# GpSimd's adds for the sums of squares, cut from one of 1280 columns into eight of 160

## The reference

```
h = rms_norm(x, norm1)
proj = h @ w_in                       # queries, keys, values, gates of three mixers
mix = concat(A(proj), B(proj), C(proj))   # sparse attention, band attention, SSD scan
x = x + mix @ w_out
u = relu(rms_norm(x, norm2) @ w_up)
x = x + (u * u) @ w_down              # d_ff = 8192
```

```
y = x32 * lax.rsqrt(jnp.mean(x32 * x32, axis=-1, keepdims=True) + EPS)
```

## Time and profile before

| | |
|---|---|
| runs, median of three | 3264.46 us |
| profiled execution, first to last instruction | 3258.3 us |
| TensorE matmul busy | 3122.3 us (96%) |
| VectorE busy | 1711.3 us (53%) |
| ScalarE busy | 1151.3 us (35%) |
| GpSimd busy | 135.7 us (4%) |
| TensorE's granted clock, mean | 0.978 |
| mean DMA rate | 136 GB/s |

### The profile page before, as it was taken

The page is one execution under the profiler, slowest core; times in us unless marked ns, Lnnn a source line. Parts: engine busy times, 40 slices in busy tenths (PEclk is TensorE's granted clock), DMA queues, the critical chain, the costliest instruction groups (busy, mean ns, idle before and its releaser), DMA issues.

```text
span 3258.3 us, 54928 instructions
## 1 busy us (share of the span) xinstructions
PE 3122.3 (96%) x20829; PEld 3064.7 (94%) x20829; DVE 1711.3 (53%) x2135; ACT 1151.3 (35%) x1376; POOL 135.7 (4%) x115
## 2 busy tenths in 40 slices
PE   6999999889999999999989999997999999999997
PEld 5899999689999999999989999986999999999997
DVE  5574467665434444444455745586644444444444
ACT  4333443233333333233323435422332333332333
POOL 4000000010000000000010000000100000000001
PEclk8999999799999999999999999997999999999999
DMA  6444443145455454454434544522454544544542
GB/s 201 125 146 126 143 143 113 57 123 146 150 150 148 148 149 149 150 150 149 130 109 131 153 143 126 155 89 64 128 151 150 149 148 148 149 150 149 150 141 79
DMA packets 233884, 444.64 MB, mean 136 GB/s; under 512 B 23073, under 2 KB 23521, under 8 KB 233425
## 3 DMA queue, kind: packets, MB, share of 16 engines
q1 hardware_dynamic: 228320, 426.37, 43.5%
q0 software_dynamic: 5424, 16.43, 1.6%
HBM read 430.94 MB, written 12.85 MB: 136 GB/s over the span
## 4 chain that ended last, share of the span: by engine, by line
PE 63%; issue 28%; DVE 5%; DVEq 1%; ACT 1%; POOLq 1%; DMA 0%; ACTq 0%; SPq 0%
PE G L682 19%; PE G L683 19%; PE G L684 19%; DVE raw_parts L1344 2%; PE M L719 1%; PE M L957 1%; PE M L851 1%; PE M L905 1%; ACT X L1043 1%; POOLq L528 0%; PE M L959 0%; DVEq L1372 0%; DVE xT L1504 0%; PE M L796 0%; PE M L777 0%
## 5 line engine op out<-in xcount | busy, mean ns | idle before, releaser
L1344 DVE TENSOR_TENSOR raw_parts<-raw,whi 128x1024 fp32r<-128x1024 f32 (+1 forms) x816 | 1013.3, 1258 | 884.5 <-ACT whi L1078 866.8
L1078 ACT ACTIVATE whi<-raw 128x1024 fp32r<-128x1024 f32 (+1 forms) x816 | 850.2, 1045 | 1469.5 <-PE G L684 1429.4
L682 PE MATMUL G<-X_parts,whi 128*128 128x320 f32 x3840 | 1200.2, 313 | 37.7 <-DVE raw_parts L1344 35.9
L684 PE MATMUL G<-X_parts,raw_parts 128*128 128x320 f32 x3840 | 1189.0, 310 | 0.0
L683 PE MATMUL G<-X_parts,whi 128*128 128x320 f32 x3840 | 1188.8, 310 | 0.0
L682 PE MATMUL G<-U_parts,whi 128*128 128x320 f32 x2560 | 805.1, 314 | 40.8 <-DVE raw_parts L1344 27.5
L683 PE MATMUL G<-U_parts,whi 128*128 128x320 f32 x2560 | 799.4, 312 | 0.0
L684 PE MATMUL G<-U_parts,raw_parts 128*128 128x320 f32 x2560 | 799.0, 312 | 0.0
L682 PEld LDWEIGHTS G<-X_parts,whi 128*128 128x128 f32 x3840 | 723.2, 188 | 44.6 <-issue 31.8
L683 PEld LDWEIGHTS G<-X_parts,whi 128*128 128x128 f32 x3840 | 723.3, 188 | 0.4
L684 PEld LDWEIGHTS G<-X_parts,raw_parts 128*128 128x128 f32 x3840 | 723.0, 188 | 0.0
(11 more groups left out here) (270 smaller groups left out, 1354.5 us busy)
## 6 DMA issues: line engine op xcount, KB each, us to landing
raw<-in_w_up SPq DMA_DIRECT2D x256, 512.0 KB, 3.7
raw<-in_w_down SPq DMA_DIRECT2D x256, 512.0 KB, 3.6
raw<-in_w_in SPq DMA_DIRECT2D x224, 512.0 KB, 3.6
raw<-in_w_out SPq DMA_DIRECT2D x64, 512.0 KB, 3.6
U<-in_x_prompt SPq DMA_DIRECT2D x2, 1024.0 KB, 7.4
out_y_prompt<-U SPq DMA_DIRECT2D x8, 256.0 KB, 2.6
bias_ext<-XC POOLq DMA_DIRECT2D x2, 768.0 KB, 5.0
raw<-in_w_in SPq DMA_DIRECT2D x16, 80.0 KB, 2.0
```

Source lines behind the costliest of these rows:

```text
L682: pe.matmul(out, hi, xh, start=(i == 0 and k == 0), stop=False)
L684: mm = pe.matmul(out, lo, xh, start=False, stop=(c == part[1] - 1 and k == KC - 1))
L1078: act.activation(whi[:, c % 4, :, cols], raw[:, c, :, cols], ACT.Copy).then_inc(high_done.sem, 1)
L1344: dve.tensor_tensor(wlo[:, c, :, cols], raw[:, c, :, cols], whi[:, c % 4, :, cols].bitcast(F32), ALU.subtract)\
```

## The change

Each of GpSimd's adds `SS4 += sq` becomes eight adds, over the four tiles and the two halves of the 320 tokens. The semaphore is counted up by the last of them. This holds for `add_squares` (sixteen times) and for the three adds at the start. The two multiplications at the start (L542, L545) stay whole.

```diff
+        def add_blocks():
+
+            for b in range(BLKS):
+                for o in range(0, TOK, TOK // 2):
+                    r = slice(o, o + TOK // 2)
+                    ins = pool.tensor_tensor(SS4[:, b, r], SS4[:, b, r], sq[:, b, r], ALU.add)
+            return ins
+
         def add_squares(l, k):
 
             pool.wait_ge(sq_done.sem, sq_done.at(l, k + 1))
-            pool.tensor_tensor(SS4[:], SS4[:], sq, ALU.add).then_inc(ss_done.sem, 1)
+            add_blocks().then_inc(ss_done.sem, 1)
             pool.drain()
...
             pool.tensor_tensor(sq, x4, x4, ALU.mult)
             pool.drain()
-            pool.tensor_tensor(SS4[:], SS4[:], sq, ALU.add).then_inc(ss_done.sem, 1)
+            add_blocks().then_inc(ss_done.sem, 1)
             pool.drain()
         pool.wait_ge(sq_done.sem, 4)
-        pool.tensor_tensor(SS4[:], SS4[:], sq, ALU.add).then_inc(ss_done.sem, 1)
+        add_blocks().then_inc(ss_done.sem, 1)
```

## The result

The changed kernel runs in 3218.86 us (median; 3212.73 to 3219.5), against 3264.49 for the one before on the same chip: a ratio of 0.9863, 95% interval 0.9852 to 0.9875. The span of the profiled execution is 3217.9 us against 3258.3, 40.4 less.

The account below looks back on a forecast made before the run. TensorE and its issue time bound the kernel; only its idle time can be won. -32.0 - 1.3 - 4.1 + 1.2 = -36.2 from span 3258.3 gives 3222.1, plus 6.2: 3228.3 us; own range 3220 to 3236, overall 3220 to 3262.

Parts of the forecast that it names:

- What bounds the kernel, and the order of turns: Whole kernel: TensorE bounds it; GpSimd and VectorE exclude each other on two-input SBUF reads, turns changing at each instruction's end.
- The 14 closings, -32.0: After unit closings, seven per layer: TensorE's stalls of 2.2 to 2.4 us for VectorE's split vanish, -32.0 us.
- Start, -4.1: Kernel start: TensorE begins at 30.0 instead of 38.47, but a new stall before chunk 3 shrinks 8.4 to -4.1 us.
- Boundary, -1.3: Layer boundary: VectorE's splits wait at most 0.5 us instead of 1.6, so TensorE resumes about 1.3 us earlier.
- End, +1.2: Kernel end: GpSimd's last add is alone on the path; VectorE's copy and the pieces' cost make it 1.2 us longer.
- Untouched stages, 0: Stages the change doesn't touch, such as mixers and scans: the forecast sum held no term for them.
- The base: Whole kernel: the forecast started from the span of 3258.3 us and added 6.2 for the median of the runs.
- A: Rival, all adds: the turn doesn't change between GpSimd's pieces, so VectorE waits for all eight; 3264.5 to 3287 us, chance 0.20.
- B: Rival, mainly closings: VectorE gets in only after several pieces; 3233, 3246 or 3260 us, chance 0.14.

Follow-up runs that it names:

- one_input: Kernel before, with each add of the closings replaced by a copy of the squares onto the sums, reading one input: 3222.10 us (one run).
- one_column: Kernel before, with the sixteen adds of the closings adding one column instead of 1280, start whole: 3212.51 us, ratio 0.9842.
- start_only: Kernel before, with only the three adds at the start cut into eight, those of the closings whole: 3257.46 us, ratio 0.9986.
- eight_again: The changed kernel once more, unaltered, measured against the kernel before on the same chip: 3215.11 us, ratio 0.9860.

## Why the prediction missed

- **What bounds the kernel, and the order of turns: right.** Stretched instructions on both sides of a closing, read as waits for each other's end, gave the cause; the bare pieces change the turn as drained ones do. One thing in it was too narrow: "when both read SBUF with two inputs" leaves out the cast and the copy with one input, which the prediction's own rows show waiting, and one_input.
- **The 14 closings, -32.0: the term that was mis-sized, and the step that failed.** The prediction took the whole loss at a closing to be the idle time in front of the first matmul, and what follows a stall to cost nothing. The closings gave 39.7 (19.86 + 19.87), where the term's far bound was 32.5. Even with every term at its far bound the sum would be 42.0 less, 3222.5. Two parts were missing. First, I took a stall from the matmul's idle time (2.23 and 2.35); the weight load in front of it had idled longer, and that is the true loss:

```profile
673.81 0.19 PEld L682 LDWEIGHTS G<-U_parts,whi 128*128 128x128 f32 x1 [2.49 <-DVE raw_parts L1344]
```

```profile
1546.49 0.19 PEld L682 LDWEIGHTS G<-U_parts,whi 128*128 128x128 f32 x1 [2.61 <-issue]
```

The kernel in which the contest costs nothing confirms both: one_column's gaps taken from those of before give 16.58 - 14.08 = 2.50 and 30.75 - 28.15 = 2.60. Eight pieces leave 0.10 and 0.20 of these, so a closing gives 2.4, 14 of them 33.5. By the matmul's rows nothing was to be left; by the weight load's, the split at 671.4 is 0.1 late (673.81 - 2.49 = 671.32). Second, 6.2 us are the clock: in each layer of the kernel before, two gaps were 1.55 longer than their neighbours. In the first of these the granted clock was down after the stall (windows of the kernel before):

```profile
704.00:708.00 4.00, 1.76 (x10) 1.50 (x9) 4.00 (x3) 1.06 (x1) 1.85 (x1) 0.89 0.57 171
708.00:712.00 4.00, 4.00 (x22) 4.00 (x21) 2.33 (x3) 0.00 (x0) 0.00 (x0) 0.69 0.03 11
```

The weight loads show it in all four long gaps: the first 12 or 13 behind the stall stand 0.27 us apart and not 0.15, which makes 13 x 0.12, about the 1.55. Behind the other ten stalls, as long as these, no load stands so far apart; why the clock fell at these four is open. One of them is the second row, whose first matmul took 0.41 as at a closing without the fall, so that row could not tell. In every kernel whose closings lose 1.14 us or less the long gaps are gone; start_only, which loses 2.5, keeps all four.
- **Start, -4.1.** It gave 6.4. TensorE's begin was right (8.7 against 8.4) and so was the new stall before chunk 3, computed for 44.9 and found at 46.02 - 1.62 = 44.4. Wrong was the old time of chunk 3, 49.0: in the kernel before chunk 0 began at the lower clock and took 4.84 us, not 3.52 (its weight loads begin at 38.46, those of chunk 1 at 43.30), so chunk 3 began at 50.3. That makes 5.9 at chunk 3, and the stage ends 6.4 ahead.
- **Boundary, -1.3.** It gave 1.9. TensorE's stall fell from 8.35 to 6.95, so the term itself was right at 1.4. Of this 0.4 went again, as more matmuls ran at the lower clock behind it; the other 0.9 came 65 to 85 us later, where TensorE idles again and the granted clock falls (0.71 and 0.60 in two windows of 5 us before, 0.81 and 0.51 after).
- **End, +1.2.** It cost 1.7, the add 1.56 of it. A piece costs 0.14 us more than its share, not 0.06: 0.48 alone, the upper bound I gave. The price from the Trainium skill (GPSIMD Engine Reference, section 7), which I had set aside for want of a row, was estimated at 0.17 and is nearer than my 0.06. The rule of section 2.1 of the same page, that a core goes on to the next instruction by itself, doesn't keep the turn from changing: the trace disagrees with what I made of it.
- **Untouched stages, 0.** They cost 4.3 us in the profiled execution (mixers and scans) and gave 3.8 in that of `eight_again` (540.3 and 538.8 for the 541.4 of before), through the clock. The sum had no term for this either way.
- **The base.** Span and time of one execution lie 1.5 us apart in the later runs of the kernel before (3261.43 and 3259.9, for one). So the 6.2 us that I added to the span were this 1.6 and an execution that was 4.6 quicker than the median, within the 3258 to 3266 that 31 later runs cover. The changed kernel's profiled execution was 0.6 slower than its median. Together they are the 5.2 between 40.4 of span and 45.6 of time; that is scatter, and no step of the prediction.

In all, the stages that the change touches gained 46.3 us where 36.2 were forecast, and 7.7 of these 10.1 came at the closings. The scan stages and the later input took 5.9 back in the profiled execution, and the base gives 5.2; that these nearly cancel, so that the miss in time is 9.4, is chance. A and B, which had 0.34 between them, came out false. The forecast's own range of 3220 to 3236, with 0.66, missed too, by size and not by mechanism.

## What to carry to other kernels

Where GpSimd and VectorE both read SBUF, an instruction's length is the length of the other's wait: cut the one off the critical path into pieces no longer than the slack of the one on it. Here the slack at a closing of a half unit is 0.38 us: sixteen pieces of 0.31 keep within it, eight of 0.48 miss it by 0.1, and four of 0.83 by 0.45. Leave the instruction whole, or in two, where it is itself the last on the path. Price a stall of TensorE by the idle time of its weight loads, and look whether the granted clock fell behind it; both told of more than the matmul's own row did. One profiled execution can lie 4.6 us off its median, as here: take the base from runs, and the differences from markers inside.

## What the hardware showed beyond that

- The turn between the two engines changes at every instruction's end, even between back-to-back instructions of GpSimd; four splits among eight pieces each waited for one piece (5.97 - 4.6 = 1.4 for four, 0.35 each, less than the 0.48 of a piece alone).
- A GpSimd memset of 1280 columns (1.18 us) neither waits for nor delays VectorE's two-input subtraction; a copy that reads one input does both (2.20 for 1.25, splits 5.68 for 4.62).
- An add of a single column waits for VectorE's subtraction just as long: it lasts 1.23 us there, 0.19 undisturbed.
- In the scan stage, where TensorE works at an uneven pace, the granted clock of the same program differs from one execution to the next, and takes or gives 4 us on the way to the next product (from 592.74 to 666.91 in one execution, from 592.80 to 662.94 in another).
